# Expert bodies of a routed feed-forward layer: first tile turned ahead, further tiles in their own body, and a class for at most 64 rows

## The reference, cut to what matters

```python
def swiglu(x, w_gu, w_d):
    g, u = jnp.split(x @ w_gu, 2, axis=-1)
    return (jax.nn.silu(g) * u) @ w_d

def moe_swiglu(x, w_router, w_gu, w_d):
    t = x.reshape(-1, D_MODEL)
    logits = (t @ w_router).astype(jnp.float32)
    top_v, top_i = lax.top_k(logits, TOP_K)
    gates = jax.nn.softmax(top_v, axis=-1)
    ...
    for e in range(N_EXPERTS):
        out = out + combine[:, e:e + 1] * swiglu(t, w_gu[e], w_d[e])
    return out.reshape(x.shape)
```

## Time and profile before

| what | value |
|---|---|
| time, median of 3 runs | 1725.15 us (1724.71 to 1725.63) |
| the profiled execution's own time | 1730.33 us |
| its span, first to last instruction | 1728.5 us |
| TensorE busy | 1636.5 us (95%) |
| VectorE busy | 1086.3 us (63%) |
| ScalarE busy | 923.3 us (53%) |
| GpSimd busy | 172.5 us (10%) |
| mean granted TensorE clock | 0.977 of full |
| the 8 experts | from about 776.9 us to 1697.6 us |

### The profile page before, as it was taken

The page is one execution under the profiler, slowest core; times in us unless marked ns, Lnnn a source line. Parts: engine busy times, 40 slices in busy tenths (PEclk is TensorE's granted clock), DMA queues, the critical chain, the costliest instruction groups (busy, mean ns, idle before and its releaser), DMA issues.

```text
span 1728.5 us, 21957 instructions
## 1 busy us (share of the span) xinstructions
PE 1636.5 (95%) x8754; PEld 1286.1 (74%) x8754; DVE 1086.3 (63%) x1205; ACT 923.3 (53%) x1130; POOL 172.5 (10%) x177
## 2 busy tenths in 40 slices
PE   5899989999999899979999999999999999999993
PEld 2577767777877687768887878887777777777772
DVE  2436663433323546658888888898988766656653
ACT  2435462322322635457777777777777555445542
POOL 2400000000000400111030302002030100010002
PEclk9899989999999999999999999999999999999997
DMA  9972326666653642329999999999999866676643
GB/s 334 295 277 98 93 90 212 227 202 198 217 197 103 217 159 74 117 89 345 383 350 379 354 364 360 351 384 350 380 348 377 285 217 207 208 230 199 215 151 124
DMA packets 295378, 421.72 MB, mean 244 GB/s; under 512 B 21458, under 2 KB 226258, under 8 KB 295152
## 3 DMA queue, kind: packets, MB, share of 16 engines
q1 hardware_dynamic: 281504, 394.85, 67.7%
q0 software_dynamic: 12624, 22.71, 4.3%
q10 hardware_dynamic: 1136, 2.64, 0.4%
HBM read 416.98 MB, written 19.27 MB: 252 GB/s over the span
## 4 chain that ended last, share of the span: by engine, by line
PE 86%; DVE 5%; DMA 5%; issue 2%; ACT 1%; POOL 0%; SPq 0%; POOLq 0%; ACTq 0%; DVEq 0%
PE ps L1394 23%; PE ps L1396 22%; PE ps L1395 22%; PE ps L1400 3%; PE ps L1401 3%; PE ps L1438 2%; PE ps L1750 2%; DMA raw<-in_w_in_dram 1%; DVE wlo L957 1%; DMA raw<-in_w_moe_gu_dram 1%; PE ps L1872 1%; ACT whi L664 1%; DMA raw<-in_w_ada_dram 1%; PE ps L1461 1%; PE ps L1418 1%
## 5 line engine op out<-in xcount | busy, mean ns | idle before, releaser
L957 DVE TENSOR_TENSOR wlo<-raw,whi 128x2048 fp32r<-128x2048 f32 x327 | 747.6, 2291 | 298.3 <-ACT whi L664 297.3
L664 ACT ACTIVATE whi<-raw 128x2048 fp32r<-128x2048 f32 x327 | 626.0, 1917 | 367.2 <-DMA raw<-in_w_ffn_gu_dram 118.8
L1394 PE MATMUL ps<-whi,xhi 128*128 128x512 f32 (+1 forms) x1352 | 544.5, 403 | 10.5 <-DVE wlo L957 5.7
L1396 PE MATMUL ps<-whi,xlo 128*128 128x512 f32 (+1 forms) x1352 | 525.5, 389 | 0.0
L1395 PE MATMUL ps<-wlo,xhi 128*128 128x512 f32 (+1 forms) x1352 | 525.4, 389 | 0.0
L1394 PEld LDWEIGHTS ps<-whi,xhi 128*128 128x128 f32 x1352 | 256.4, 190 | 82.8 <-DVE wlo L957 19.1
L1396 PEld LDWEIGHTS ps<-whi,xlo 128*128 128x128 f32 x1352 | 256.1, 189 | 53.9
L1395 PEld LDWEIGHTS ps<-wlo,xhi 128*128 128x128 f32 x1352 | 256.7, 190 | 46.8 <-issue 0.5
L1394 PE MATMUL ps<-whi,hhi 128*128 128x512 f32 x484 | 197.3, 408 | 3.0 <-DVE wlo L957 2.6
L1396 PE MATMUL ps<-whi,hlo 128*128 128x512 f32 x484 | 190.4, 393 | 0.0
L1395 PE MATMUL ps<-wlo,hhi 128*128 128x512 f32 x484 | 190.0, 393 | 0.0
(11 more groups left out here) (226 smaller groups left out, 1275.8 us busy)
## 6 DMA issues: line engine op xcount, KB each, us to landing
raw<-in_w_moe_gu_dram SPq DMA_DIRECT2D x352, 512.0 KB, 7.0
raw<-in_w_moe_d_dram SPq DMA_DIRECT2D x176, 512.0 KB, 5.9
raw<-in_w_ada_dram SPq DMA_DIRECT2D x96, 512.0 KB, 4.9
raw<-in_w_in_dram SPq DMA_DIRECT2D x44, 512.0 KB, 5.4
raw<-in_w_ffn_gu_dram SPq DMA_DIRECT2D x44, 512.0 KB, 8.2
raw<-in_w_ffn_d_dram SPq DMA_DIRECT2D x22, 512.0 KB, 7.5
raw<-in_w_out_dram SPq DMA_DIRECT2D x16, 512.0 KB, 4.0
bias<-rpb_rows POOLq DMA_DIRECT2D x32, 96.0 KB, 5.1
```

What stands on the lines that cost most here:

```text
L664: act.activation(whi[m % SPL][:, :], raw[n % RING][:, :], ACT.Copy).then_inc(s_hi, 1)
L957: dve.tensor_tensor(wlo[n % RING][:, :], raw[n % RING][:, :], whi[NTH[n] % SPL][:, :].bitcast(F32), ALU.subtract).then_inc(s_lo, 1)
L1394: pe.matmul(out, a_hi, w_hi, start=start, stop=False)
L1396: return pe.matmul(out, a_lo, w_hi, start=False, stop=stop)
```

## The change

**A fifth shape.** `SHAPES` begins with (0, 1): no full tile, one half tile, for at most 64 rows. The half tile's code, which stood fast on tile 1 before, goes by T. VectorE counts one more threshold for `ntile`. A branch at the end of a body now has four comparisons in place of three, and the first shape in the code is (0, 1): on the way to an expert 0 with another shape the engines branch.

**Rows.** `gathered` is gone. In its place `first_rows` turns only the first tile of the next expert, after down chunks 2 and 3, four pieces at a time. The further tiles (`more_rows`) are turned at the start of the expert's own body, and only as many as its shape has. GpSimd gathers the first tile of expert e+2 as before, but waits for only the first two turns, and gathers the further tiles after it has scattered expert e, once body e+1 has turned its own.

```diff
-SHAPES = [(1, 0), (1, 1), (2, 0), (3, 0)]
+SHAPES = [(0, 1), (1, 0), (1, 1), (2, 0), (3, 0)]
...
             for e in range(NE):
                 if e + 2 < NE:
                     pool.wait_ge(s_ga, KT * (e + 2))
-                    rows_of(e + 2)
+                    rows_of(e + 2, 0)
...
+                if e + 2 < NE:
+                    pool.wait_ge(s_mored, MORE * (e + 2))
+                    pool.wait_ge(s_hxm, 16 * (NT - 1) * (e + 1))
+                    for i in range(1, NT):
+                        rows_of(e + 2, i)
...
-                        act.activation(under[0:HALF, 0:512], ps[HALF:P, 2 + b % 2, :], ACT.Copy).then_inc(s_under, 1)
+                        act.activation(under[0:HALF, 0:512], ps[HALF:P, 2 * T + b % 2, :], ACT.Copy).then_inc(s_under, 1)
...
+            def more_rows(T, half, e):
+                if T + half < NT:
+                    act.sem_inc(s_morea, 2 * (NT - T - half))
+                for t, i in further(T, half):
+                    act.wait_ge(s_more, nth_more(T, half, e, t, i))
+                    act.activation(xhi[:, 4 * i:4 * i + 4, P * t:P * t + P],
+                                   ps[:, 6 + i, :].rearrange("p (k n) -> p k n", k=4), ACT.Copy).then_inc(s_morea, 1)
...
+                more_rows(T, half, e)
                 state["n"] = n0 + 2
                 gate_up(T, e + 1, lambda j: n0 + j, n0 + N_GU + 2, half)
                 for q in range(FK // 2):
                     upto(n0 + N_GU + q + 2)
-                    if e < NE - 1 and 2 <= q < 2 + KT:
-                        gathered(e + 1, q - 2)
+                    if e < NE - 1 and 2 <= q < 4:
+                        first_rows(e + 1, q - 2)
...
-            chain(dve.tensor_scalar(cnt[:, :], ps[:, 3, 0:NE], float(P), None, ALU.is_gt))
+            chain(dve.tensor_scalar(cnt[:, :], ps[:, 3, 0:NE], float(HALF), None, ALU.is_gt))
+            chain(dve.scalar_tensor_tensor(out=cnt[:, :], in0=ps[:, 3, 0:NE], scalar=float(P), in1=cnt[:, :],
+                                           op0=ALU.is_gt, op1=ALU.add))
...
+            def first_rows(e, i):
+                if i == 0:
+                    pe.wait_ge(s_hx, 16 * e)
+                for j in range(4):
+                    kt = 4 * i + j
+                    ins = pe.transpose(ps[:, 6 + i, P * j:P * j + P], hx[:, 0, P * kt:P * kt + P], ident[:, :])
+                ins.then_inc(s_ga, 4)
```

More of the change, by code:

```diff
@@ L422, in __call__, with further, nth_more @@
                 self.eng.wait_ge(self.s, self.n)
+        MORE = 2 * (NT - 1)
+        def further(T, half):
+            return [(t, i) for t in range(1, T + half) for i in range(2)]
+        def nth_more(T, half, e, t, i):
+            return MORE * e + 2 * (NT - T - half) + 2 * (t - 1) + i + 1
         def tiles_of(eng, e):
@@ L625, in _, with rows_of @@
             pool.wait_ge(s_scat, 16 * 2 * NT)
[L627 to L634, removed]
+            def rows_of(e, i):
+                pool.indirect_dma_start(out=hx[:, i, :], out_offset=None, in_=h_rows[:, :],
+                                        in_offset=bass.IndirectOffsetOnAxis(ap=lidx[:, e, i:i + 1], axis=0),
+                                        bounds_check=N_ROWS - 1, oob_is_err=False
+                                        ).then_inc(s_hxm if i else s_hx, 16)
+            for i in range(NT):
+                rows_of(1, i)
             for e in range(NE):
@@ L770, in gate_up @@
                         act.wait_ge(s_sum, (GU_B + 1) * (k - 1) + b + 1)
-                        ins = act.activation(pg[0:HALF, 1, :], under[0:HALF, 512:768], ACT.Silu)
+                        ins = act.activation(pg[0:HALF, T, :], under[0:HALF, 512:768], ACT.Silu)
                     ins.then_inc(s_sg, 1)
@@ L813, in expert @@
                 if half:
-                    act.activation(under[0:HALF, :], ps[HALF:P, 2:4, :].rearrange("p a n -> p (a n)"), ACT.Copy
+                    b = 2 * (NT - 1 - T)
+                    act.activation(under[0:HALF, :], ps[HALF:P, b:b + 2, :].rearrange("p a n -> p (a n)"), ACT.Copy
                                    ).then_inc(s_under, 1)
@@ L1114, in expert @@
                 state["n"] = n0 + 2
-                if e == 0 and T + half > 1:
-                    for kt in range(KT):
-                        picked_more(kt, P * (T - 1) + HALF * half)
-                    dve.wait_ge(s_mored, KT)
+                more_rows(T, half, e)
                 if half:
-                    dve.wait_ge(s_glo, KT * (e + 1))
-                    dve.tensor_copy(xhi[:, :, P + HALF:2 * P], xlo[:, :, P:P + HALF].bitcast(F32)).then_inc(s_pack, 1)
+                    if T:
+                        dve.wait_ge(s_mored, MORE * (e + 1))
+                    else:
+                        dve.wait_ge(s_glo, KT * (e + 1))
+                    dve.tensor_copy(xhi[:, :, P * T + HALF:P * T + P], xlo[:, :, P * T:P * T + HALF].bitcast(F32)
+                                    ).then_inc(s_pack, 1)
                 else:
@@ L1775, in gate_up @@
                             if b == 0 and h == 0:
-                                free(1)
+                                free(T)
                                 pe.wait_ge(s_pack, k)
@@ L1879, in free @@
                 def free(t):
-                    pe.wait_ge(s_glo, KT * (e + 1))
+                    if t == 0:
+                        pe.wait_ge(s_glo, KT * (e + 1))
+                    else:
+                        pe.wait_ge(s_mored, nth_more(T, half, e, t, 1))
                     if e:
@@ L1884, in between @@
                 def between(q):
-                    if e < NE - 1 and 2 <= q < 2 + KT:
-                        if q < 4:
-                            pe.wait_ge(s_hlo, (e + 2) * 2 * GU_B)
-                        gathered(e + 1, q - 2)
-                if e == 0 and T + half > 1:
-                    for kt in range(KT):
-                        picked_more(kt, P * (T - 1) + HALF * half)
-                    pe.wait_ge(s_mored, KT)
+                    if e < NE - 1 and 2 <= q < 4:
+                        pe.wait_ge(s_hlo, (e + 2) * 2 * GU_B)
+                        first_rows(e + 1, q - 2)
+                more_rows(T, half, e)
                 gate_up(T, e + 1, lambda j: n0 + j, free, half)
```

100 lines of the change are left out of this document (49 added, 51 removed).

## The result

The changed kernel takes 1781.58 us (median of 4, 1780.49 to 1784.2) against 1725.39 us: a ratio of 1.0325, 95% interval 1.0307 to 1.0343, or 56 us more. The forecast was 1773 us in a range of 1753 to 1796. The profiled execution took 1784.2 us, its span is 1782.5.

A forecast was written before the change was run, and what follows sets the result against it. TensorE and the weight loads were taken to bind together before, a ScalarE-VectorE ring in (0, 1) after. 35.6 + 10.4 + 2.6 - 2.6 + 2 = +48 us, from 1725.15 to about 1773 us, range 1753 to 1796.

The forecast's parts named there:

- The ring: In a (0, 1) block, ScalarE and VectorE wait on each other in turn: 7.6 us a block in place of 5.72.
- The first three steps: In a (0, 1) block: ScalarE's split until VectorE's 1.93 us, VectorE's two splits 4.42, addition of halves to ScalarE 0.72.
- the other signs that the prediction named: Changed trace: bodies 1 and 5 some 115 us, DMA well under 1, TensorE half busy, 4 to 5 us stalls.
- Which experts: By gathered rows, experts 1 and 5 take (0, 1); 0, 2, 3, 4 keep (1, 0); 6, 7 keep (1, 1).
- The bodies of (0, 1): Bodies 1 and 5: entry 6.5, loop 83.8, tail 24.8, sum 115.1 us against 97.3; +35.6 us for both.
- The branches: Shape changes into experts 0, 2 and 6 stall the engines: +3, +5.3 and +2.1, in all +10.4 us.
- The further tiles: Expert 7's turns, copies and subtractions now stand behind body 6's result, ahead of an awaited cast: +2.6 us (0.9 to 3.5).
- The fewer turns: Less TensorE work in down of bodies 0, 2, 3, 4, 6, counted mainly for 0: -2.6 us (0 to -9).
- Faster: Rival: no costly ring, blocks under 5.7 us, bodies 1 and 5 load-bound, branches free: about 1711 us; chance 0.04.
- Half clock throughout: Rival: TensorE's clock stays at half in (0, 1), 8.1 us a block: about 1815 us; chance 0.08.
- Branches nearly free: Rival: the ring holds, but five stalls of 3 to 5 us fall away: 1755 us; chance 0.13.
- the forecast's +2 for the clock: TensorE in (0, 1) partly at half clock, with the ring nearly the bound: +2 us in all.

The follow-up runs named there:

- the kernel without the class: The changed kernel without the shape for at most 64 rows (experts 1 and 5 in (1, 0)), moved turns kept: 1725.92 us, ratio 0.9986.
- the kernel with the full tile: The changed kernel with the class for at most 64 rows kept, but its body computing like (1, 0): 1734.41 us, ratio 1.0037.

## Why the prediction was right, and where it was off

**The ring held to the step.** Forecast: 7.6 us a block, ScalarE waiting about 2.8 us for the addition, VectorE about 1.5 us for the split. Measured: 7.73, 2.74 and 1.48. The first three steps came out as forecast (1.94, 4.41 and 0.72 us); the 0.13 us is in the last ones, 0.44 us from the silu to the `hhi` copies in place of 0.33, and 0.22 from there to the next split in place of 0.2. Loop: 83.8 us forecast, 11 x 7.73 = 85.0 measured. That it is a ring, and not a sum of work, is shown three ways: one split moved out of it takes 37 us away, an addition in it adds its 0.60 us to every period, a copy beside it adds nothing. Of the other signs that the prediction named, two came out otherwise. TensorE is busy for 72% of the stretch and not half of it, since part of its matmuls run at half clock. And ScalarE did not stand 4 to 5 us at all five changes of shape: 4.64, 0.16, 3.56, 5.42 and 8.87 us.

**Which experts.** Right: bodies 1 and 5 have the half tile's instructions (L788, L1096), no other body of at most 128 rows has.

**The bodies of (0, 1), +35.6 forecast, +43 measured.** Counted on TensorE, from the end of its last matmul of one body (its start and 0.23 us) to that of the next, body 1 takes 118.4 us and body 5 119.9, against 97.3 and 98.1. (The table's 45 us hold 2 us more, since ScalarE's copies start late there.) Of body 1, 15.7 us lie before the second block's first split, ten blocks take 77.3, and the tail 25.4; of body 5, 15.8, 77.3 and 26.8. Forecast were 14.1 (6.5 and one block), 76 and 24.8. So three terms were each a little small, and the entry had another reason than was forecast: TensorE waited 6.53 us in all for VectorE's cast, before which VectorE had stood for 4.33, then ran its first chunk at half clock, and ScalarE's second split waited for that chunk to be done. The clock's cost was spread over the blocks in the forecast, where the ring hides it, and it falls at the entries. In the tail the forecast had ruled the loads out, but in the changed kernel splits of the last chunks waited for them:

```profile
1402.54 1.92 ACT L681 ACTIVATE whi<-raw 128x2048 fp32r<-128x2048 f32 x1 [1.84 <-DMA raw<-in_w_moe_d_dram]
1405.55 1.91 ACT L681 ACTIVATE whi<-raw 128x2048 fp32r<-128x2048 f32 x1 [1.10 <-DMA raw<-in_w_moe_gu_dram]
```

**The branches, +10.4 forecast, +10.9 measured** (expert 0 +2.0, 2 +4.1, 6 +4.8, counted the same way). The sum is near, in part by luck. What the moved turns gain stands in the same three bodies; against the kernel without the class, which has those gains too, they cost 13.9 us (2.8, 4.6 and 6.5). The steps were partly wrong as well. Forecast for expert 2 was that ScalarE and VectorE come late for chunk 2, 7.5 us less 2.2 given back. What happened is that TensorE itself stood, 5.46 us before its first matmul, and ran at half clock after it, so that chunk 2 was ready in time. That the loads give back part of a stall was right: 1.9 of 3.8 us in the kernel with the full tile.

What the profile names as the end of TensorE's 5.46 us is VectorE's increment behind its addition (L1151). It was not that. In the six kernels that leave a body (0, 1), TensorE stands 5.40 to 5.49 us before body 2, while its first matmul comes anything from 0.02 to 1.02 us after the end of that addition. In the kernel with the addition between the splits it is 0.02 us, and the profile names nothing:

```profile
977.61 0.76 PE L1414 MATMUL ps<-whi,xhi 128*128 128x512 f32 x1 [5.49 <-issue]
```

So this stall is TensorE's own. Why it is some 1.6 us longer than the 3.90 of the kernel with the full tile stays open.

**The further tiles, +2.6 forecast, +2.7 measured** for expert 7, and here, too, the agreement is partly luck. TensorE's wait for the cast grew by only 1.0 us, from 1.17 to 2.17. The rest fits the granted clock, for which this term had nothing. The first 9.7 us of expert 7 (columns as in rows 2), in the kernel without the class and in the kernel with the full tile, whose code is the same there:

```profile
1520.30:1530.00 9.70, 7.53 (x32) 5.92 (x31) 5.22 (x5) 6.07 (x6) 4.52 (x3) 0.87 0.57 182
...
1536.80:1546.50 9.70, 7.53 (x38) 6.06 (x36) 5.22 (x5) 6.55 (x6) 4.53 (x3) 1.00 0.60 191
```

With the same wait of 2.17 us before them, TensorE's matmuls fall to half clock for some 3 us in the one and stay at full in the other, and expert 7 takes 166.2 and 164.6 us. The changed kernel is of the first kind, at a clock of 0.82.

**The fewer turns, -2.6 forecast, about -3.1 measured,** if experts 0 to 6 of the kernel without the class are added up in the table. The size was about right and the place was not: most was forecast for expert 0, which gained 0.8 us, and half of it came in expert 6, for which nothing was counted. Differences of 0.6 us and less between single traces are weak evidence.

**The rivals.** "Faster" fell, since a block is 7.73 us and not under 5.7. "Half clock throughout" fell: the clock did go to half in parts of the blocks (0.81 over the stretch), as feared, but the ring and not TensorE ends the waits. The rule of the Trainium skill, "TensorE: Matmul & The Clock Gate", section "HAM oscillation — how this bites in real kernels", describes what was seen, the clock falling again and again between short bursts; its price here was nil inside the ring. "Branches nearly free" is not so far off as its chance of 0.13 said: 2.2 us each.

**The sum.** Forecast +48, measured +56. The bodies of (0, 1) make nearly all of the difference. They were 8.1 us longer than forecast (the entries 3.3, the blocks 2.6, the tails 2.6, less 0.4 of rounding), and added 7.3 us more, since body 5 took 98.1 us before and not 97.3; the forecast's +2 for the clock covers part of it. 42.9 for these bodies, 10.9 at the changes of shape and 2.7 for expert 7 are 56.5, and experts 3 and 4 give 0.2 back.

## What to carry to other kernels

When a change takes work off the busiest engine by giving a small step to two others, write their queues for one round side by side and go round from wait to wait: if the path comes back to its start, that sum is the new period, and the engines' busy shares say nothing of it. In a ring the order of two instructions can be worth more than all the work that was saved: 37 us here for moving one addition ahead of one split. And a shape of its own for few cases costs a branch into it and one out of it each time, which has to be won back first.

## What the runs showed of the hardware

- At a branch to another shape's body each engine has its own stall, and not the same one. In the kernel with a full tile in the class TensorE stood 3.65 to 3.93 us at each change of shape. ScalarE stood 4.40 us on the way to expert 0, 0.16 on the way to 1, none that the profile shows to 2, and 5.47 to 5. VectorE's first work of bodies 1 and 2 came 1.63 and 1.56 us after its last, and it waited for ScalarE in that time, while in the changed kernel it stood 4.33 us on the way to body 1. Why some of them were free no run tells.
- A stall of 3.8 to 3.9 us on TensorE cost 1.9 to 2.0 us in bodies 1 and 2 of that kernel, where the loads bind as well, although some 3 us at half clock followed it: ScalarE's waits for the weights fell from 15.5 to 2.6 us.
- After an idle time of 6.53 us TensorE's matmuls started 0.43 us apart for some 5 us, half clock (1.2 GHz), and 0.23 us after that. In blocks in which it worked in short bursts the mean granted clock was 0.81, with four more matmuls a chunk 0.94, and with the addition between the splits, blocks 6.04 us apart, 1.00. After a wait of 2.17 us at the same place it fell in one kernel and not in another.
